# A decoder step on one core: half of the interleaved conditioning weights go to an unsplit stream behind the recurrent gates

## The chip, the cores and the metric

The kernel runs on one core of a Trainium2 chip. The metric is the device time of one execution in microseconds (us). The engines have these names: PE is TensorE's matmul side and PEld its weight loads; DVE is VectorE, ACT is ScalarE, POOL is GpSimd, and SP is the queue that issues most DMAs. An instruction waits on semaphores, and its engine's queue is held until they are reached.

## The reference

One layer of a hybrid decoder on 1024 prompt rows and 64 sample rows (8 sequences of 8), model width 1024. The part that the change touches is the conditioning and the mixer around it:

```python
mod = silu(c) @ w_ada + b_ada            # 9 rows of c, 6*1024 columns
sh_m, sc_m, gt_m, sh_f, sc_f, gt_f = split(mod, 6)
h = rms_norm(x, g_mix) * (1 + sc_m) + sh_m
u_val, u_glu, u_rec, u_y = split(h @ w_in + b_in, 4)
ca = causal_dwconv(u_val * sigmoid(u_glu), width 31)
ya = silu(layer_norm(ca))
cb = causal_dwconv(u_rec, width 4)
hb = rg_lru(cb)                          # two block-diagonal gates, then a scan over time
x = x + gt_m * (concat[ya, hb * gelu(u_y)] @ w_out)
x = x + gt_f * (relu(h2 @ w_up)**2 @ w_down)   # h2 uses sc_f and sh_f
```

The new states of both convolutions and of the recurrence are outputs too.

## The kernel before, in words

Rows of x are tokens in 9 tiles of 128; inside the mixer data is transposed, channels on the partitions and 1088 tokens along the free axis, cut in three chunks of 384, 384 and 320. A float32 product is made from three products of a high and a low part ("split"): ACT copies the raw piece to its high part, POOL subtracts to get the low part, PE multiplies.

The order on every engine is written out by hand; engines meet at semaphores. The program has an opening (norms, the first four of twelve groups of 512 `w_ada` columns, transposes), then **eight steps** of `w_in`, then the **variance stage** of the layer norm, then the **recurrence**, then the output product over 9 tiles, then eight blocks of the MLP.

A step m takes two strips of 128 `w_in` columns (s = 0 and 1), each in three chunks c: 24 products a chunk (PE lines 1472 to 1474 in `strip`). Between the chunks PE does the **conditioning**: one later group of 512 `w_ada` columns a step, in four pieces (`ada_piece`, lines 1364 and 1365, four products of 512 columns each). Each piece is loaded by SP (line 276), copied by ACT (line 590) and subtracted by POOL (line 376). When a group is complete, ACT copies its rows out (`group_rows`, line 576), PE turns them in a product with nine columns (`group_turn`, line 1372), and ACT adds the bias into `mod` (`group_out`, line 581). DVE meanwhile runs the width-31 convolution, one channel tile after another (line 1169), then the width-4 one (line 1146). In the last step PE also forms the mean over channels (`mean`, line 1480).

In the variance stage ACT squares the centred values (`squares`, line 789), PE averages them (line 1480 again, `var_a`) into banks 6 and 7 of PSUM, and ACT takes the root (line 795). In the recurrence PE forms two gates for each of four channel tiles (`recurrent_gates`, line 1567), ACT applies tanh, exp and tanh (`recurrence`, lines 800 to 812), and PE, between them, transposes the convolutions' tails (`turn_state`, line 1557) that ACT copies out (`staged`, line 817). POOL makes low parts of `w_out` and squares of the decay (line 461). PE then turns the mixer's gate rows (`gates`, lines 1589 and 1593) and waits for the first output product (`tile_product`, line 1614), which needs all of the split `ya` and `yb` from ACT and DVE (lines 1243 to 1254). SP loads `w_out` in eight pieces, each after the low part of the piece before it in its slot.

## Time and profile before

| what | value |
|---|---|
| three runs, median (lowest to highest) | 1296.15 us (1293.26 to 1296.56) |
| the profiled execution, its own time | 1296.5 us |
| its span | 1294.7 us |
| PE busy; DVE; ACT; POOL | 92%; 56%; 31%; 29% |
| mean granted clock of PE | 0.957 |

The span is what the trace shows; 1.8 us of the profiled execution lie outside it. PE is busy nearly throughout, but busy time says nothing of the clock: PEclk is the granted clock, 1.00 for 2.4 GHz and 0.50 for 1.2 GHz.

### The profile page before, as it was taken

What the parts mean: (1) busy time and instruction counts of PE and PEld (TensorE: products, weight loads), DVE (VectorE), ACT (ScalarE), POOL (GpSimd) and SP (SyncE); (2) the same over time, 40 slices, a digit from 0 to 9 for tenths busy, and PEclk for the clock granted to TensorE, in tenths of its full rate; (3) what the DMA queues carried; (4) which work ended last, traced back from release to release, by engine and by line L of the source; (5) the groups of instructions that cost most, each with busy time, mean ns of one, the idle gap of its engine ahead of it and who ended that gap; (6) DMA issues with size and microseconds to landing.
All of it is one profiled execution on the core that took longest, in us unless ns stands there. A gap on an engine that the chain in (4) does not pass through costs nothing.

```text
span 1294.7 us, 16511 instructions
## 1 busy us (share of the span) xinstructions
PE 1192.5 (92%) x6175; PEld 1068.0 (82%) x6175; DVE 723.8 (56%) x809; ACT 402.8 (31%) x704; POOL 369.3 (29%) x217
## 2 busy tenths in 40 slices
PE   6798999999723999899999999999999999999996
PEld 2687999997423888888998998998988988988985
DVE  2649699996686455524534534535535435435447
ACT  4752334433791433420320320320310310311322
POOL 0246777652453010410320410410410311311300
PEclk9697999999966999899999999999999999999998
DMA  9533343321204110210210210310300300201102
GB/s 298 163 98 98 98 126 117 109 86 49 68 32 151 37 33 1 82 50 1 78 53 1 81 49 0 90 40 0 97 32 0 97 32 10 87 32 32 49 33 105
DMA packets 74661, 87.26 MB, mean 67 GB/s; under 512 B 3816, under 2 KB 53248, under 8 KB 74627
## 3 DMA queue, kind: packets, MB, share of 16 engines
q1 hardware_dynamic: 72448, 85.21, 21.1%
q10 hardware_dynamic: 2179, 1.61, 0.5%
q8 instruction: 20, 0.33, 0.1%
q14 instruction: 14, 0.11, 0.0%
HBM read 81.72 MB, written 5.08 MB: 67 GB/s over the span
## 4 chain that ended last, share of the span: by engine, by line
PE 85%; DVE 5%; SPq 2%; ACT 2%; POOL 2%; DMA 1%; issue 1%; ACTq 0%; DVEq 0%; POOLq 0%
PE ps L1472 15%; PE ps L1474 14%; PE ps L1473 14%; PE ps L1614 11%; PE ps L1615 11%; PE ps L1617 11%; PE ps L1480 1%; PE ps L1621 1%; PE ps L1620 1%; SPq L265 1%; PE ps L1365 1%; PE ps L1364 1%; DVE tmp_a L1235 1%; DMA x<-in_x_prompt 1%; DVE ga L1232 1%
## 5 line engine op out<-in xcount | busy, mean ns | idle before, releaser
L1472 PE MATMUL ps<-act_hi,w_hi 128*128 128x384 f32 (+1 forms) x1152 | 381.0, 331 | 8.0 <-DVE act_lo L1048 3.9
L1473 PE MATMUL ps<-act_lo,w_hi 128*128 128x384 f32 (+1 forms) x1152 | 378.4, 328 | 0.0
L1474 PE MATMUL ps<-act_hi,w_lo 128*128 128x384 f32 (+1 forms) x1152 | 378.3, 328 | 0.0
L1472 PEld LDWEIGHTS ps<-act_hi,w_hi 128*128 128x128 f32 x1152 | 218.7, 190 | 11.0 <-issue 4.8
L367 POOL TENSOR_TENSOR wb_lo<-raw,wb_hi 128x1024 fp32r<-128x1024 f32 x40 | 99.9, 2506 | 430.0 <-ACT wb_hi L568 403.3
L367 POOL TENSOR_TENSOR w_lo<-raw,w_hi 128x1024 fp32r<-128x1024 f32 x48 | 118.4, 2468 | 363.8 <-ACT w_hi L568 305.7
L1272 DVE TENSOR_TENSOR ps<-ps,gt_p 128x1024 f32<-128x1024 f32 x72 | 88.7, 1233 | 237.6 <-PE ps L1617 237.6
L1473 PEld LDWEIGHTS ps<-act_lo,w_hi 128*128 128x128 f32 x1152 | 218.8, 190 | 1.6
L1474 PEld LDWEIGHTS ps<-act_hi,w_lo 128*128 128x128 f32 x1152 | 218.6, 190 | 0.0
L1614 PE MATMUL ps<-wb_hi 128*128 128x512 f32 x512 | 199.4, 389 | 1.1 <-ACT gt_s L899 1.1
L1615 PE MATMUL ps<-wb_lo,wb_hi 128*128 128x512 f32 x512 | 199.2, 389 | 0.0
L1302 DVE TENSOR_TENSOR relu<-relu 128x384 f32<-128x384 f32 (+1 forms) x96 | 74.7, 778 | 199.3 <-ACT relu L942 199.3
L1617 PE MATMUL ps<-wb_hi,wb_lo 128*128 128x512 f32 x512 | 157.7, 389 | 0.0
L568 ACT ACTIVATE wb_hi<-raw 128x1024 fp32r<-128x1024 f32 x40 | 41.3, 1051 | 364.9 <-PE ps L1621 319.2
L1169 DVE SCALAR_TENSOR_TENSOR ps<-ga,caw,ps 128x1024 f32<-128x1024 f32 x112 | 134.2, 1282 | 0.0
L1614 PEld LDWEIGHTS ps<-wb_hi 128*128 128x128 f32 x512 | 96.1, 188 | 21.1 <-ACT gt_s L899 1.3
L1617 PEld LDWEIGHTS ps<-wb_hi,wb_lo 128*128 128x128 f32 x512 | 96.1, 188 | 20.0
L1615 PEld LDWEIGHTS ps<-wb_lo,wb_hi 128*128 128x128 f32 x512 | 96.1, 188 | 19.7
L942 ACT ACTIVATE relu<-ps 128x384 f32<-128x384 f32 (+1 forms) x96 | 45.2, 471 | 187.6 <-PE ps L1474 178.5
L1274 DVE TENSOR_TENSOR x<-x,ps 128x1024 f32<-128x1024 f32 x72 | 87.9, 1221 | 2.5
L1614 PE MATMUL ps<-wb_hi,act_hi 128*128 128x512 f32 x128 | 51.3, 401 | 39.9 <-DVE stk L1254 39.9
L376 POOL TENSOR_TENSOR aw_lo<-raw_ada,aw_hi 128x1024 fp32r<-128x1024 f32 x32 | 80.2, 2523 | 17.7 <-ACT aw_hi L590 17.7
(224 smaller groups left out, 1298.9 us busy)
## 6 DMA issues: line engine op xcount, KB each, us to landing
raw_ada<-in_w_ada SPq DMA_DIRECT2D x32, 512.0 KB, 3.7
raw<-in_w_up SPq DMA_DIRECT2D x32, 512.0 KB, 4.0
raw<-in_w_down SPq DMA_DIRECT2D x32, 512.0 KB, 3.3
ada<-in_w_ada SPq DMA_DIRECT2D x8, 1024.0 KB, 15.0
x<-in_x_prompt SPq DMA_DIRECT2D x16, 512.0 KB, 8.8
raw<-in_w_in SPq DMA_DIRECT2D x16, 512.0 KB, 4.8
raw<-in_w_out SPq DMA_DIRECT2D x8, 512.0 KB, 3.4
out<-x SPq DMA_DIRECT2D x8, 512.0 KB, 2.6
```

The costliest lines, as they stand in the source:

```text
L367: pool.tensor_tensor(dst, raw[:, slot, :], hi.bitcast(F32), ALU.subtract).then_inc(lo_ready, 1)
L376: pool.tensor_tensor(aw_lo[:, slot, :], raw_ada[:, slot, :], aw_hi[:, slot, :].bitcast(F32), ALU.subtract).then_inc(ada_lo, 1)
L1169: dve.scalar_tensor_tensor(out=out if k == KA - 1 else a, in0=win, scalar=w, in1=a, op0=ALU.mult, op1=ALU.add).then_inc(conva_tap, 1)
L1272: dve.tensor_tensor(src, src, gt_p[:, :], ALU.mult).then_inc(gated, 1)
L1274: dve.tensor_tensor(x2[:, t, :], x2[:, t, :], src, ALU.add).then_inc(rmw_done, 1)
L1302: dve.tensor_tensor(f, r, r, ALU.mult).then_inc(r2_done, 1)
L1472: mm(out, wh, xh, start=(k == 0), stop=False)
L1473: mm(out, wh, xl, start=False, stop=False)
L1474: last = mm(out, wl, xh, start=False, stop=(k == KD - 1))
L1614: mm(out, ah, wh, start=(k == 0), stop=False)
L1615: mm(out, ah, wl, start=False, stop=False)
L1617: last = mm(out, al, wh, start=False, stop=end)
```

## The change

Eight `w_ada` groups were split and interleaved with steps 0 to 7. Now four are: their pieces run one step later (group m-1 in step m, steps 1 to 4, and its turn in the step after). The last four groups, which give the MLP's scale and gate rows, are loaded unsplit in sixteen chunks of 128 columns into a buffer that lies where the strips' high and low weights were, and multiplied as float32 with nine columns each, straight into PSUM bank 7 (`late_piece`): two chunks between the recurrent gates, fourteen behind them. One DVE instruction adds their bias. The squares go to other memory and the first stands in the last step; each variance chunk has a bank of its own; the tails all go through bank 6; the loops over the steps are unrolled.

```diff
+ADA_S = 4
+LATE = ADA_G - ADA0 - ADA_S
+ROW_L = 4 * (ADA0 + ADA_S)
...
-        rs = shared([("h_st", [9, WA], F32)], [("w_hi", [P, 2, D], F32R)])
-        h_st, w_hi = rs["h_st"], rs["w_hi"]
-        w_lo = sb("w_lo", [P, 2, D], F32R)
+        rs = shared([("h_st", [9, WA], F32)], [("ada_late", [P, 4, KD, P], F32)],
+                    [("w_hi", [P, 2, D], F32R), ("w_lo", [P, 2, D], F32R)])
+        h_st, ada_late, w_hi, w_lo = (rs[n] for n in ("h_st", "ada_late", "w_hi", "w_lo"))
...
-        xsq = tmp_b[:, 0:J, :]
+        xsq = lru
...
+            for m in range(2 * J):
+                if m < 2 * J - 1:
+                    nxt, apart = ((m + 1) * P, WA) if m < J - 1 else (2 * WA + (m + 1 - J) * 2 * P, P)
                     for s in range(2):
-                        load_piece(2 * m + s + 1, s, win_v[:, :, bass.ds(nxt + s * apart, P)], True)
-                load_ada(m, 2)
-                load_ada(m, 3)
-                if nxt is not None:
-                    load_ada(m + 1, 0)
-                    load_ada(m + 1, 1)
-
-            with sp.Fori(0, J - 1) as j:
-                step(j, (j + 1) * P)
-            step(J - 1, 2 * WA, P)
-            with sp.Fori(0, J - 1) as j:
-                step(j + J, (j + 1) * (2 * P) + 2 * WA, P)
-            step(2 * J - 1, None)
-            for k in range(KD):
+                        load_piece(2 * m + s + 1, s, win_v[:, :, nxt + s * apart:nxt + s * apart + P], True)
+                if 0 < m <= ADA_S:
+                    load_ada(m - 1, 2)
+                    load_ada(m - 1, 3)
+                if m < ADA_S:
+                    load_ada(m, 0)
+                    load_ada(m, 1)
+
+            def load_late(a):
+
+                for i in range(4):
+                    wait(sp, late_used, 4 * (a - 1) + i + 1)
+                    at = (ADA0 + ADA_S + a) * GW + i * P
+                    sp.dma_start(ada_late[:, i, :, :], wada_v[:, :, at:at + P]).then_inc(late_in[i], 16)
+
+            def load_out(k):
                 load_piece(W_OUT0 + k - 1, k % 2, w_out[0, k * P:(k + 1) * P, :], False)
+
+            load_out(0)
+            load_out(1)
+            sp.wait_ge(strip_a, 2 * J * NC)
+            sp.wait_ge(strip_b, 2 * J * NC)
+            load_late(0)
+            for k in range(2, 6):
+                load_out(k)
+            for a in range(1, LATE):
+                load_late(a)
+            load_out(KD - 2)
+            load_out(KD - 1)
...
+            def step(m):
+                if m < 2 * J - 1:
...
+                if 0 < m <= ADA_S:
+                    split_ada(4 * m - 2, 0)
+                    split_ada(4 * m - 1, 1)
...
-                    pool.wait_ge(ada_evac, ADA_G)
-                    for g, row0 in ((0, M_GTM), (1, M_GTF)):
-                        for k in range(KD):
-                            last = pool.tensor_copy(gt_tok[:, g, k, :].rearrange("p (b t) -> p b t", t=TB),
-                                                    mod[:, row0 + k, 1:9].unsqueeze(2).broadcast_to([P, NB, TB]))
-                    last.then_inc(tails, 1)
-                    pool.wait_ge(ada_tr, ADA_G)
-                    pool.wait_ge(st_tr, 1)
+                    pool.wait_ge(ada_tr, ADA0 + ADA_S)
+                    pool.wait_ge(ada_evac, ADA0 + ADA_S)
+                    sample_gate(0, M_GTM)
...
+            pool.wait_ge(late_mod, 1)
+            sample_gate(1, M_GTF)
...
+                def out_b(c, bank):
+                    if last and c == 2:
+                        squares(0)
+                    gelu_out(c, bank, 2 * q + 1, evac_b)
+                step(q + J + J // 2, out_a, out_b)
...
-                act.activation(rstd[:, t0:t0 + w], ps[:, 6 + c % 2, 0:w], ACT.Sqrt, bias=eps[:, :]).then_inc(sd_done, 1)
+                act.activation(rstd[:, t0:t0 + w], ps[:, 5 + c, 0:w], ACT.Sqrt, bias=eps[:, :]).then_inc(sd_done, 1)
...
-            squares(0)
             squares(1)
             squares(2)
-            act.wait_ge(ada_lo, 4 * 2 * J)
-            w_out_hi(0)
             for c in range(NC):
                 deviation(c)
+            w_out_hi(0)
             w_out_hi(1)
+            recurrence(0)
             staged(0, stage[0:KA - 1, 2, :], 6, KA - 1)
             act.dma_start(ca_prompt[0, 0], stage[0:KA - 1, 2, :]).then_inc(staged_out, 16)
             staged_a(0)
-            recurrence(0)
+            recurrence(1)
             staged_a(1)
-            staged(3, stage[64:64 + KB - 1, 2, :], 7, KB - 1)
+            w_out_hi(2)
+            recurrence(2)
+            staged(3, stage[64:64 + KB - 1, 2, :], 6, KB - 1)
             act.dma_start(cb_prompt[0, 0], stage[64:64 + KB - 1, 2, :]).then_inc(staged_out, 16)
-            recurrence(1)
-            w_out_hi(2)
+            w_out_hi(3)
+            recurrence(3)
             staged(4, stage[32:32 + NB * (KB - 1), 2, :], 6, NB * (KB - 1))
             act.dma_start(cb_sample[0].rearrange("b s c -> (b s) c"),
                           stage[32:32 + NB * (KB - 1), 2, :]).then_inc(staged_out, 16)
...
+            dve.wait_ge(late_used, 4 * LATE)
+            b_late = par[:, C_BADA + ROW_L:C_BADA + 48].unsqueeze(2).broadcast_to([P, 48 - ROW_L, 9])
+            dve.tensor_tensor(mod[:, ROW_L:48, :], ps[:, 7, 0:9 * (48 - ROW_L)].rearrange("p (r c) -> p r c", c=9),
+                              b_late, ALU.add).then_inc(late_mod, 1)
+            dve.wait_ge(ada_evac, ADA0 + ADA_S)
+            dve.wait_ge(late_mod, 1)
             scales(sc_f, M_SCF, C_GFFN)
...
             def var_a(c):
                 pe.wait_ge(sq_done, c + 1)
                 if c == 1:
-                    pe.wait_ge(ada_evac, ADA_G)
-                if c == 2:
-                    pe.wait_ge(sd_done, 1)
-                mean(c, 6 + c % 2, lambda j: xsq[:, j, c * CH:c * CH + CW[c]], var_done)
-
-            def step(m, last=False, late=()):
+                    pe.wait_ge(ada_evac, ADA0 + ADA_S)
+                mean(c, 5 + c, lambda j: xsq[:, j, c * CH:c * CH + CW[c]], var_done)
...
-                        if c == 0 and s == 0:
-                            for i in late:
-                                ada_piece(m - 1, i)
-                            group_turn(m + ADA0 - 1, 7, 0)
-                        for i in ((), (2 * s,), (2 * s + 1,))[c]:
-                            ada_piece(m, i)
+                        if isinstance(m, int) and s == 0 and c == 0 and 2 <= m <= ADA_S + 1:
+                            group_turn(ADA0 + m - 2, 7, 0)
+                        if isinstance(m, int) and c > 0 and m <= ADA_S:
+                            ada_piece(m - 1, 2 * s + c - 1)
...
+            for m in range(1, 2 * J - 1):
                 step(m)
             step(2 * J - 1, True)
...
-                wait(pe, st_cp, n - 1)
+                wait(pe, st_cp, n)
...
+            def late_piece(a, i):
+
+                pe.wait_ge(late_in[i], 16 * (a + 1))
+                at = 36 * a + 9 * i
+                for k in range(KD):
+                    last = mm(ps[:, 7, at:at + 9], ada_late[:, i, k, :], c_t[:, k, :],
+                              start=(k == 0), stop=(k == KD - 1))
+                last.then_inc(late_used, 1)
+
             for c in range(NC):
                 var_a(c)
             pe.wait_ge(sd_done, NC)
             pe.wait_ge(tails, 1)
+            recurrent_gates(0)
             turn_state(0, 6, KA - 1, lambda j: tail_p[:, j, :])
-            turn_state(1, 7, 4 * (KA - 1), lambda j: tail_a[:, j, 0:120])
-            recurrent_gates(0)
+            turn_state(1, 6, 4 * (KA - 1), lambda j: tail_a[:, j, 0:120])
+            recurrent_gates(1)
+            late_piece(0, 0)
             turn_state(2, 6, 4 * (KA - 1), lambda j: tail_a[:, j, 120:240])
+            recurrent_gates(2)
+            late_piece(0, 1)
             pe.wait_ge(tails, 2)
-            turn_state(3, 7, KB - 1, lambda j: tail_bp[:, j, :])
-            recurrent_gates(1)
+            turn_state(3, 6, KB - 1, lambda j: tail_bp[:, j, :])
+            recurrent_gates(3)
             turn_state(4, 6, NB * (KB - 1), lambda j: tail_b[:, j, :])
-            recurrent_gates(2)
-            recurrent_gates(3)
+            for q in range(2, 4 * LATE):
+                late_piece(q // 4, q % 4)
...
-            gates(M_GTM, 4, 6)
+            gates(M_GTM, 4, 2)
...
+                    pe.wait_ge(tails, 4)
                     gates(M_GTF, 6, 4)
...
```

On PE, from the last recurrent gate to the first output product, before (L1567 is a recurrent gate, L1557 a tail's transpose, L1589 and L1593 the gate turns, L1614 the output product):

```order
L1567 MATMUL ps<-ga,wg 128x384 [waits evac_a,convb_tap]
L1567 MATMUL ps<-ga,wg 128x384 [waits evac_a]
L1567 MATMUL ps<-ga,wg 128x320 [waits evac_a]
L1567 MATMUL ps<-ga,wg 128x384 [waits evac_b] x2
L1567 MATMUL ps<-ga,wg 128x320 [waits evac_b]
L1589 MATMUL ps<-ident,mod 128x128 [waits st_cp,tails,evac_b,evac_a]
L1589 MATMUL ps<-ident,mod 128x128 x7
L1593 MATMUL ps<-ident,gt_tok 64x128 x8
L1614 MATMUL ps<-wb_hi,act_hi 128x512 [waits yal_done,hi_ready,yah_done,lo_ready,ylo_done,yhi_done]
```
and in the changed program (there L1566, L1556, L1601, L1605 and L1626; L1574 is a late chunk's eight products):

```order
L1566 MATMUL ps<-ga,wg 128x384 [waits evac_b] x2
L1566 MATMUL ps<-ga,wg 128x320 [waits evac_b]
L1556 MATMUL ps<-ident,tail_b 24x128 [waits st_cp]
L1556 MATMUL ps<-ident,tail_b 24x128 x3
L1574 MATMUL ps<-c_t,ada_late 128x9 [waits late_in2]
L1574 MATMUL ps<-c_t,ada_late 128x9 x7
```
The last late chunk and what follows it, in the changed program:

```order
L1574 MATMUL ps<-c_t,ada_late 128x9 [waits late_in3]
L1574 MATMUL ps<-c_t,ada_late 128x9 x7
L1601 MATMUL ps<-ident,mod 128x128 [waits st_cp,tails,evac_b,evac_a]
L1601 MATMUL ps<-ident,mod 128x128 x7
L1605 MATMUL ps<-ident,gt_tok 64x128 x8
L1626 MATMUL ps<-wb_hi,act_hi 128x512 [waits yal_done,hi_ready,yah_done,lo_ready,ylo_done,yhi_done]
```

Fourteen late chunks, of which the first and the last stand here, have come between the last recurrent gates and the gate turns; each chunk waits for its own load.

On ACT, the end of the last step and the variance stage, before (L677 moves the end of a strip's last chunk out, L576 and L581 are the group's rows, L789 squares, L795 is the root, L568 a high part of `w_out`):

```order
L677 ACTIVATE gel<-ps,par 128x64
L576 ACTIVATE ada_rows<-ps 128x512 [waits ada_used]
L581 ACTIVATE mod<-ps,par 128x9 [waits ada_tr]
L581 ACTIVATE mod<-ps,par 128x9 x3
L789 ACTIVATE tmp_b<-conv_a 128x4x384 [waits ada_used,xc_done,strip_b,k_done]
L789 ACTIVATE tmp_b<-conv_a 128x4x384 [waits xc_done]
L789 ACTIVATE tmp_b<-conv_a 128x4x320 [waits xc_done]
L568 ACTIVATE wb_hi<-raw 128x1024 [waits raw_in0,ada_lo]
L795 ACT_TABLE_LOAD
L795 ACTIVATE rstd<-ps,eps 128x384 [waits var_done] x2
L795 ACTIVATE rstd<-ps,eps 128x320 [waits var_done]
L568 ACTIVATE wb_hi<-raw 128x1024 [waits raw_in1]
```
and in the changed program (there L688 and L689, L770, L801 and L580):

```order
L686 ACTIVATE gel<-ps,par 128x384 [waits strip_b] x2
L770 ACTIVATE lru<-conv_a 128x4x384 [waits ada_used,xc_done,strip_b]
L688 ACTIVATE gel<-ps,par 128x256
L689 ACTIVATE gel<-ps,par 128x64
L770 ACTIVATE lru<-conv_a 128x4x384 [waits ada_used,xc_done,k_done]
L770 ACTIVATE lru<-conv_a 128x4x320 [waits ada_used,xc_done]
L801 ACT_TABLE_LOAD
L801 ACTIVATE rstd<-ps,eps 128x384 [waits var_done] x2
L801 ACTIVATE rstd<-ps,eps 128x320 [waits var_done]
L580 ACTIVATE wb_hi<-raw 128x1024 [waits raw_in0]
L580 ACTIVATE wb_hi<-raw 128x1024 [waits raw_in1]
```
The group's rows are gone from the front of the squares. The first square stands ahead of the last move out of a strip, and carries that move's wait for the strip. Both high parts of `w_out` now follow the roots.

On SP, the loads behind the steps, before (L271 is a load of `w_in` or `w_out`, L265 the reload of x):

```order
L276 DMA raw_ada<-in_w_ada 128x2x512 [waits ada_lo] x2
L271 DMA raw<-in_w_out 128x1024 [waits lo_ready] x8
L265 DMA x<-in_x_prompt 128x1024 [waits yah_done,yal_done,ylo_done,yhi_done]
L265 DMA x<-in_x_prompt 128x1024 x7
L265 DMA x<-in_x_sample 64x1024
L271 DMA raw<-in_w_up 128x8x128 [waits lo_ready] x2
```
and in the changed program (there L276 and L270; L313 is a late chunk):

```order
L276 DMA raw<-in_w_out 128x1024 [waits lo_ready] x2
L313 DMA ada_late<-in_w_ada 128x8x128 [waits strip_b,strip_a]
L313 DMA ada_late<-in_w_ada 128x8x128 x3
L276 DMA raw<-in_w_out 128x1024 [waits lo_ready] x4
L313 DMA ada_late<-in_w_ada 128x8x128 [waits late_used] x12
L276 DMA raw<-in_w_out 128x1024 [waits lo_ready] x2
L270 DMA x<-in_x_prompt 128x1024 [waits yah_done,yal_done,ylo_done,yhi_done]
L270 DMA x<-in_x_prompt 128x1024 x7
L270 DMA x<-in_x_sample 64x1024
```
Four late chunks stand behind the first two pieces of `w_out`, and twelve ahead of its last two.

## Rows read from the trace of the kernel before

**Rows 1.** windows by stage: us, busy of each engine (x instructions), PEclk, DMA share, GB/s.
```profile
core 0 of [0], span 1294.7 us
...
139.00:316.50 177.50, 177.50 (x1033) 170.31 (x1031) 161.46 (x134) 64.39 (x118) 116.76 (x75) 1.00 0.33 98
...
368.00:408.00 40.00, 0.38 (x4) 0.14 (x2) 39.06 (x37) 23.34 (x32) 19.00 (x12) 0.54 0.08 26
```

**Rows 2.** timeline of PE at the first step after the opening: start, us, what [idle before].
```profile
98.25 0.66 PE L1472 MATMUL ps<-act_hi,w_hi 128*128 128x384 f32 x1 [3.81 <-ACT w_hi L746]
...
111.33 1.88 PE L1372 MATMUL ps<-pick,ada_rows 128*128 128x9 f32 x8 [4.97 <-ACT ada_rows L576]
...
113.06 0.67 PE L1472 MATMUL ps<-act_hi,w_hi 128*128 128x384 f32 x1
```

**Rows 3.** timeline of PE inside step 1, then the group turns of steps 2 and 3.
```profile
124.26 0.39 PE L1364 MATMUL ps<-aw_hi,stk 128*128 128x512 f32 x1
...
125.19 0.34 PE L1472 MATMUL ps<-act_hi,w_hi 128*128 128x384 f32 x1
...
143.10 0.95 PE L1372 MATMUL ps<-pick,ada_rows 128*128 128x9 f32 x8
...
143.91 0.43 PE L1472 MATMUL ps<-act_hi,w_hi 128*128 128x384 f32 x1
...
171.47 0.95 PE L1372 MATMUL ps<-pick,ada_rows 128*128 128x9 f32 x8
```

**Rows 4.** timeline of DVE, the starts of two tiles of the long convolution.
```profile
147.68 1.35 DVE L1161 TENSOR_SCALAR ps<-ga,caw,par 128x1024 f32 x1 [11.26 <-POOL ga L393]
...
188.94 1.35 DVE L1161 TENSOR_SCALAR ps<-ga,caw,par 128x1024 f32 x1 [0.79 <-DVE conv_a L1172]
```

**Rows 5.** chain that ended last, start, us, what: a mean product of the last step.
```profile
291.15 2.58 PE ps L1480 x8
```

**Rows 6.** timeline of ACT from the last strip to the first gate.
```profile
315.79 0.47 ACT L676 ACTIVATE gel<-ps,par 128x256 f32<-128x256 f32 x1 [3.86 <-PE ps L1474]
...
319.08 4.03 ACT L789 ACTIVATE tmp_b<-conv_a 128x1536 f32<-128x1536 f32 x3
...
331.29 0.53 ACT L795 ACTIVATE rstd<-ps,eps 128x320 f32<-128x320 f32 x1 [1.57 <-PE ps L1480]
...
331.71 1.05 ACT L568 ACTIVATE wb_hi<-raw 128x1024 fp32r<-128x1024 f32 x1
...
334.74 1.28 ACT L800 ACT_TABLE_LOAD   x1 [0.46 <-PE ps L1567]
...
336.04 0.90 ACT L800 ACTIVATE tmp_a<-ps,hb 128x768 f32<-128x768 f32 x1
```

**Rows 7.** windows of PE's clock, columns as in the first group.
```profile
40.00:42.00 2.00, 2.00 (x12) 2.00 (x11) 2.00 (x3) 2.00 (x6) 0.00 (x0) 0.50 1.12 353
...
110.00:112.00 2.00, 0.67 (x4) 0.67 (x4) 2.00 (x3) 1.75 (x3) 2.00 (x3) 0.50 0.98 256
...
408.00:412.00 4.00, 3.77 (x9) 3.03 (x10) 0.28 (x2) 0.00 (x0) 0.00 (x0) 0.50 0.71 255
```

**Rows 8.** timeline of PE, the gate turns and the first output product.
```profile
361.55 3.75 PE L1589 MATMUL ps<-ident,mod 128*128 128x128 f32 x16 [4.38 <-ACT tmp_a L803]
...
365.24 3.14 PE L1593 MATMUL ps<-ident,gt_tok 128*64 128x128 f32 x16
...
408.23 0.77 PE L1614 MATMUL ps<-wb_hi,act_hi 128*128 128x512 f32 x1 [39.85 <-DVE stk L1254]
```

**Rows 9.** page section 6, loads of 512-byte runs: KB each, us to landing.
```profile
raw<-in_w_in SPq DMA_DIRECT2D x16, 512.0 KB, 4.8
```

**Rows 10.** a window in which one such load lands; columns as in the first group.
```profile
642.00:643.00 1.00, 1.00 (x9) 1.00 (x8) 0.83 (x1) 0.97 (x3) 1.00 (x1) 1.00 1.14 343
```

**Rows 11.** timeline of DVE, start and end of the recurrence's last part.
```profile
367.71 1.29 DVE L1232 SCALAR_TENSOR_TENSOR ga<-tmp_a,ga 128x1088 f32<-128x1088 f32 x1
...
407.92 0.21 DVE L1254 TENSOR_TENSOR stk<-gel,stk 128x64 fp32r<-128x64 f32 x1
```

135 lines of the change are left out of this document (54 added, 81 removed).

## The prediction

> **What bounds the kernel now.** I read the page's slices first, then the chain of work that ended last, then windows by stage, and last the timelines of PE, ACT and DVE around each join. The span is 1294.7 us; the profiled execution took 1296.5 us, so 1.8 us lie outside the span, and it is 0.35 us above the median of the runs. The sum below is made against 1296.5.
>
> From 139 to 316.5 us PE is busy for all of the 177.5 us, at a granted clock of 1.00: the steps are bound by PE, and an instruction taken out of PE's row there comes off the end [rows 1]. From 368 to 408 us it is the other way round: PE does nothing, DVE is busy for 39.06 of 40 us, and PE's first output product then follows an idle time of 39.85 us that a DVE write of `stk` ended [rows 1, 8]. So there are two bounds, PE in the steps and the chain through ACT, POOL and DVE in the recurrence. Behind 408 us the edit touches only small waits (the MLP's gate rows), and I take that part as unchanged.
>
> **The steps.** One piece of conditioning is four products, which hold PE from 124.26 to 125.19, so a piece costs 0.93 us. A group's turn, eight records for four products, takes from 143.10 to 143.91, which is 0.81 us. The turns of steps 2 and 3 lie 28.37 us apart, so a step without pieces and turn is 28.37 - 4 x 0.93 - 0.81 = 23.84 us, and its first chunk (384 of 2 x 1088 columns) about 4.2 us [rows 3].
>
> Step 1 now begins at 98.25 us behind an idle time of 3.81 us [rows 2]. Two pieces that stood ahead of that idle time move away, but the wait is for the low part of the weights, which POOL makes behind the first gate product; so I leave the start at 98.25. Before, PE ran out of conditioning pieces in this step, sat idle for 4.97 us for ACT's group rows, and turned them at half rate (the next product is 1.73 us later) [rows 2]. Its step 2 began about 4.2 us ahead of 143.10, at 138.9. After the change step 1 holds four pieces, whose splits have been ordered long before, and no turn: 23.84 + 3.72 = 27.6 us, and I allow 3.5 us for a slow beginning, since PE's clock stood at 0.50 after the similar idle time at 110 us [rows 7]. That gives 129.3 instead of 138.9: **9.6 us**. Bounds: 0 to 6 us for the slow beginning.
>
> Steps 2 to 4 keep four pieces and a turn. Step 5 keeps its turn. Steps 5, 6 and 7 lose four pieces each, 11.2 us, and steps 6 and 7 a turn each, 1.6 us; one piece of these stood behind the last chunk, so the last chunk ends 11.9 us earlier by that. Before, ACT moved it out at 315.79 [rows 6]; now at 315.8 - 9.6 - 11.9 = **294.3**. Can DVE follow? A tile of the long convolution takes 41.26 us, and before the first two were parted by 11.26 us of waiting [rows 4]. With the product of step 1 some 9 us earlier the four tiles close up, and the last ends near 138 + 3 x 41.26 = 262 instead of 147.68 + 3 x 41.26 = 271.5. The mean in step 7 then asks for it at 294.3 less five chunks and the means, near 271. So DVE isn't late, with some 9 us to spare. Unrolling can gain nothing, since PE had no gaps at the loops' ends; I price it at 0, and at most 2 us of loss.
>
> **The variance stage.** Before, from the last move-out to the first tanh it was 336.04 - 315.79 = 20.25 us [rows 6]. The change puts the first square ahead of that move, but the order rows show that it carries the wait for the last chunk, so the square begins in the last step in name only; its 4.03 / 3 = 1.34 us stand behind the chunk [rows 6]. Then three averages at the rate of the mean in step 7, 2.58 us each at most [rows 5], run without waiting for one another's bank, one root 0.53, two high parts of `w_out` at 1.05, and a table load of 1.28 [rows 6]: 1.34 + 7.74 + 0.53 + 2.1 + 1.28 = 13.0 us. The first tanh comes at 307.3, which is 28.7 us earlier. If the averages run at half rate as they did before, 3 to 7 us of that are lost.
>
> **The recurrence, by the y chain.** Before, the last part on DVE began at 367.71, 31.7 us behind the first tanh, and ended at 408.1 [rows 6, 11]. Each tail now goes through bank 6 and waits for the copy of the one before: a round trip on ACT and PE, some 0.5 us each, five times. POOL, on the other side, copies eight gate rows there and not sixteen. I take the two as equal, with -2 to +2.4 us around it. By this chain the first output product would come at 408.2 - 28.7 = 379.5.
>
> **The recurrence, by the late chunks.** The same PE row now holds sixteen chunks, 14 of them between the last gates and the gate turns. A chunk is eight products of nine columns. At full rate it costs 2 x 0.81 = 1.62 us [rows 3]. At half rate, from the group's turn at 111.33 to the next product at 113.06, it costs 2 x 1.73 = 3.46 us [rows 2]. Which rate will be granted is the largest unknown of this sum. At 40 to 42 us PE was busy for all of 2 us, with transposes, at 0.50, and at 110 to 112 us, when a turn began behind idle time, it was at 0.50 too [rows 7]. The turns at full rate stand inside dense strips [rows 3]. The chunks come behind gates with gaps between them, so I take **half rate**, 3.46 us, and keep 1.62 as the other end.
>
> The Trainium skill (TensorE: Matmul & The Clock Gate, section Why this matters for your kernels) asks to keep TensorE busy without gaps to have the full rate, and by that a run of fourteen chunks should be at 2.4 GHz; the window from 40 to 42 us, busy throughout at 0.50, does not agree, and no run here shows a long row of nine-column products. By that rule the result would be the first rival below.
>
> PE ended its last gate at 361.55 - 4.38 = 357.2, which is 21.1 us behind the first tanh [rows 6, 8]. Two chunks now stand between the gates and partly fill its gaps; I take 26 us, so the run starts at 333.3. Fourteen chunks of 3.46 are 48.4 us: 381.7. The loads keep up: one of 512 KB in 512-byte runs takes 4.8 us to land in the median, but its bytes pass at up to 343 GB/s, 1.5 us each with several under way, and four are under way [rows 9, 10]. SP issues the second four behind the sixth piece of `w_out`, which waits for POOL's fourth low part, near the start of the run. The gate turns take 365.24 + 3.14 - 361.55 = 6.8 us [rows 8]: **388.5**. The last two pieces of `w_out` stand behind the late loads in SP's queue, which wait until the twelfth chunk is used, at 333.3 + 10 x 3.46 = 368; they land near 374, and behind them ACT's last `yb` parts and DVE's end near 381, ahead of the turns' end.
>
> **The sum.** The first output product moves from 408.2 to 388.5: 19.7 us. Before, it started cold, at 0.50 from 408 to 412 us [rows 7]; behind the turns it should start warm, which saves about 1.7 us. 1296.5 - 19.7 - 1.7 = 1275.1, and against the median of the runs 1275.
>
> **Rivals.**
> 1. *The late chunks hide.* They run at full rate; 14 x 1.62 = 22.7 us end near 356, and the y chain sets the start at 379.5, cold. Time: 1296.5 - 28.7 = 1268; with the recurrence shorter by 2, 1266. For it: a turn inside a step takes 0.81 us [rows 3]. Against it: the windows at 0.50 [rows 7].
> 2. *The loads pace the run.* They land 4.8 us apart [rows 9]. The twelve behind SP's late issue, at about 334, land until 392; with one chunk and the turns 402.4, so 1296.5 - 5.8 - 1.7 = 1289. Against it: 343 GB/s in the window [rows 10].
> 3. *Slower.* The loads come strictly one at a time, each behind the use of the chunk before: 4.8 + 3.46 = 8.3 us by twelve, 99 us from 334, and the turns: 440. The product starts 32 us late: 1327. It decides from 5.6 us a chunk on ((408.2 - 6.8 - 334) / 12). Against it: four buffers, four semaphores, and SP waits only for the use of the chunk four places back.
> 4. *It does not do what it says.* The steps stay as long as they were because something else than PE sets them (DVE's convolution, the weights' low parts). Then only the variance stage's 7 us are won: the run starts at 336 - 7 + 26 = 355, and with 48.4 and 6.8 us the first product comes at 410, so about no change, 1296. Against it: PE's 177.5 of 177.5 us [rows 1].
>
> **How the numbers follow.** A time within 0.3% of before (4 us) can't be told from no change here. Forecast 0.60, rival 1 0.24, rival 2 0.08, rival 3 0.03, rival 4 0.03, and 0.02 for faster still. The forecast's own range, from the slow beginning, the averages' rate and the start of the run, is 1269 to 1282. The range that holds 8 in 10 takes rival 1 in and stops at rival 2: 1264 to 1288. Faster 0.94, within 0.3% 0.03, slower 0.03.
>
> **What would show it.** In the changed profile: no wait for group rows in step 1, and steps 5 to 7 near 24 us each; the last strip's end near 294; the first square behind it; the first tanh near 307; the fourteen chunks in one run at a granted clock of 0.50 and 3.5 us each; the gate turns directly behind them and the first output product directly behind the turns, with no DVE wait ahead of it. Wrong if the first output product still waits for `stk` (then rival 1), if PE waits for late loads between chunks (2 or 3), or if the last strip ends later than 300.

## The result and the profile after

The changed kernel takes 1271.9 us (median of four runs, 1271.63 to 1273.25) against 1296.4 us (1293.26 to 1296.93): a ratio of 0.9818, with a 95% interval of 0.9801 to 0.9835. The forecast was 1275. The profiled execution has a span of 1270.0 us, 24.7 less than before; the difference is made ahead of the first output product, as a table by step shows (us from the span's start).

| step | before | forecast | measured |
|---|---|---|---|
| step 2 of `w_in` begins | 138.9 | 129.3 | 128.5 |
| last chunk of the steps is out of PE | 315.8 | 294.3 | 293.3 |
| first tanh of the recurrence | 336.0 | 307.3 | 306.2 |
| the row of late chunks begins | | 333.3 | 329.8 |
| it ends | | 381.7 | 380.3 |
| last `stk` of the y chain written | 408.1 | 379.5 | 380.6 |
| first output product | 408.2 | 388.5 | 385.6 |
| from there to the end of the span | 886.5 | 884.8 | 884.4 |

The first tanh comes 29.8 us earlier. The first output product comes only 22.6 us earlier: 7.2 us are given back in the recurrence, where PE's row is now the longest. 2.1 us more lie behind the first output product, which now starts at full clock (its first record takes 0.50 us, against 0.77 before [rows 8]). Together 24.7.

Timeline of PE in the changed kernel (start, us, engine, line, what, number of records, [idle before <- what ended it]); it answers to [rows 2, 3, 8]:

```profile
98.80 0.66 PE L1481 MATMUL ps<-act_hi,w_hi 128*128 128x384 f32 x1 [5.70 <-POOL w_lo L383]
...
128.53 0.34 PE L1481 MATMUL ps<-act_hi,w_hi 128*128 128x384 f32 x1
...
311.89 1.11 PE L1556 MATMUL ps<-ident,tail_a 128*120 128x128 f32 x4 [4.48 <-ACT stage L823]
...
317.69 1.85 PE L1574 MATMUL ps<-c_t,ada_late 128*128 128x9 f32 x16
...
329.78 4.52 PE L1574 MATMUL ps<-c_t,ada_late 128*128 128x9 f32 x32
339.20 41.13 PE L1574 MATMUL ps<-c_t,ada_late 128*128 128x9 f32 x192 [4.90 <-DMA ada_late<-in_w_ada]
380.18 3.62 PE L1601 MATMUL ps<-ident,mod 128*128 128x128 f32 x16
383.73 1.96 PE L1605 MATMUL ps<-ident,gt_tok 128*64 128x128 f32 x16
385.62 0.50 PE L1626 MATMUL ps<-wb_hi,act_hi 128*128 128x512 f32 x1
```

Read it from below. The first output product has no idle time before it: it follows the gate turns, and these follow the late chunks, where before it had waited 39.85 us for DVE [rows 8]. A chunk is 16 records. Two chunks took 4.52 us; then PE stood still for 4.90 us for a load, and twelve more took 41.13 us, 3.43 each.

Timeline of ACT, same columns, which answers to [rows 6]:

```profile
293.25 1.48 ACT L770 ACTIVATE lru<-conv_a 128x1536 f32<-128x1536 f32 x1 [2.93 <-PE ps L1483]
294.64 0.46 ACT L688 ACTIVATE gel<-ps,par 128x256 f32<-128x256 f32 x1
...
306.20 0.90 ACT L806 ACTIVATE tmp_a<-ps,hb 128x768 f32<-128x768 f32 x1
...
372.29 1.06 ACT L580 ACTIVATE wb_hi<-raw 128x1024 fp32r<-128x1024 f32 x1 [14.18 <-DMA raw<-in_w_out]
```

The first square does stand ahead of the last move-out, and PE's last chunk released it. At 372.29 ACT gets the seventh piece of `w_out` behind 14.18 us of waiting. Timeline of DVE, which answers to [rows 11]: one product of the recurrence for the first and for the third channel tile, 1.29 and 3.28 us, and the end of the chain.

```profile
338.44 1.29 DVE L1236 SCALAR_TENSOR_TENSOR ga<-tmp_a,ga 128x1088 f32<-128x1088 f32 x1
...
349.78 3.28 DVE L1236 SCALAR_TENSOR_TENSOR ga<-tmp_a,ga 128x1088 f32<-128x1088 f32 x1
...
380.36 0.21 DVE L1258 TENSOR_TENSOR stk<-gel,stk 128x64 fp32r<-128x64 f32 x1
```

The change did not make the third one long. In the kernel before it was the same:

```profile
379.04 3.27 DVE L1232 SCALAR_TENSOR_TENSOR ga<-tmp_a,ga 128x1088 f32<-128x1088 f32 x1
```

Windows of the changed kernel (stretch; length; busy time of PE, PEld, DVE, ACT, POOL; granted clock; DMA share; GB/s), which answer to [rows 1, 7]:

```profile
139.00:290.00 151.00, 151.00 (x888) 146.32 (x887) 145.45 (x131) 44.83 (x86) 76.98 (x59) 1.00 0.23 67
...
330.00:332.00 2.00, 2.00 (x20) 2.00 (x19) 0.34 (x1) 1.97 (x3) 2.00 (x6) 1.00 0.00 0
332.00:334.00 2.00, 2.00 (x13) 2.00 (x12) 0.00 (x0) 1.97 (x3) 2.00 (x2) 0.58 0.01 4
...
350.00:360.00 10.00, 10.00 (x49) 10.00 (x48) 9.72 (x8) 8.05 (x12) 5.71 (x4) 0.50 0.55 159
...
384.00:386.00 2.00, 2.00 (x18) 1.78 (x17) 0.00 (x0) 1.13 (x2) 0.00 (x0) 1.00 0.89 328
```

PE is still busy in all of the steps. In the row of late chunks it is busy too, for 10.00 of 10.00 us, and yet the clock is at 0.50 (1.2 GHz). It was still at 1.00 from 330 to 332 us, with the first chunk of the row, fell while the second one ran and PE was busy, and came back only in the gate turns.

### The profile page after: what moved, and what is told of

It reads as the page before. It is cut to its first block, busy times and chain, and to the rows that moved or that the text cites. A ratio compares the mean times of both kernels' runs of the same rounds, so it can differ in the third digit from the quotient of the medians.

```text
span 1270.0 us, 16342 instructions
## 1 busy us (share of the span) xinstructions
PE 1212.0 (95%) x6335; PEld 1094.6 (86%) x6335; DVE 708.1 (56%) x810; ACT 382.5 (30%) x668; POOL 326.9 (26%) x201
## 4 chain that ended last, share of the span: by engine, by line
PE 90%; DVE 2%; SPq 2%; ACT 2%; DMA 1%; issue 1%; POOL 0%; ACTq 0%; DVEq 0%; POOLq 0%
PE ps L1481 15%; PE ps L1483 15%; PE ps L1482 15%; PE ps L1626 11%; PE ps L1629 11%; PE ps L1627 11%; PE ps L1574 4%; PE ps L1633 1%; PE ps L1632 1%; PE ps L1489 1%; SPq L270 1%; PE ps L1566 1%; DMA x<-in_x_prompt 1%; SPq L276 1%; PE ps L1374 1%
## 5 line engine op out<-in xcount | busy, mean ns | idle before, releaser
L1626 PE MATMUL ps<-wb_hi 128*128 128x512 f32 x512 | 199.4, 389 | 1.1 <-ACT gt_s L903 1.1
L580 ACT ACTIVATE wb_hi<-raw 128x1024 fp32r<-128x1024 f32 x40 | 41.2, 1051 | 375.0 <-PE ps L1633 319.3
L1626 PEld LDWEIGHTS ps<-wb_hi 128*128 128x128 f32 x512 | 96.1, 188 | 21.1 <-ACT gt_s L903 1.3
L1316 DVE TENSOR_TENSOR wb_lo<-relu,wb_hi 128x384 fp32r<-128x384 f32 (+1 forms) x96 | 51.5, 536 | 7.6 <-ACT stk L952 4.0
L1574 PEld LDWEIGHTS ps<-c_t,ada_late 128*128 128x128 f32 x256 | 49.4, 302 | 5.3 <-DMA ada_late<-in_w_ada 5.0
```

The source lines that it names most:

```text
L1574: last = mm(ps[:, 7, at:at + 9], ada_late[:, i, k, :], c_t[:, k, :], start=(k == 0), stop=(k == KD - 1))
L1626: mm(out, ah, wh, start=(k == 0), stop=False)
```

## The experiments

Each kernel is the changed one with the edit shown. Ratios are to the kernel before, as above (the changed kernel: 0.9818).

**The gate turns behind the fourth chunk.** The theory under test is that PE's row sets the first output product.

```diff
-            for q in range(2, 4 * LATE):
-                late_piece(q // 4, q % 4)
...
-            gates(M_GTM, 4, 2)
+            for q in range(2, 4 * LATE):
+                if q == 4:
...
+                    gates(M_GTM, 4, 2)
+                late_piece(q // 4, q % 4)
```

> The gate turns stand in PE's row behind the fourth late chunk, where PE now waits 4.90 us for loads, and no longer behind the sixteenth. My theory: PE's row of late chunks and turns sets the first output product. The turns can begin once ACT has copied the last tails, near 335.4, and take 5.4 to 6.8 us, so they fill that wait; the twelve chunks (41.1 us) then end near 382 and the first output product follows there, not at 385.6: the time is 1272 - 3.6 = 1268, and the product stands directly behind a chunk. Rival: the y chain sets it (the last stk at 380.4 in the changed kernel was only waiting for nothing better); then the product stays near 385 and the time at 1272. Second rival: the turns, whose products have 128 columns, bring the clock back to 1.00 for the chunks behind them; then the twelve chunks take 20 us and the product waits for stk, at about 380: 1266 or less.

Measured: 1268.4 us, ratio 0.9789 (0.9773 to 0.9806). Timeline of PE:

```profile
335.22 3.75 PE L1598 MATMUL ps<-ident,mod 128*128 128x128 f32 x16 [1.73 <-ACT stage L823]
338.90 2.76 PE L1602 MATMUL ps<-ident,gt_tok 128*64 128x128 f32 x16
341.59 38.98 PE L1574 MATMUL ps<-c_t,ada_late 128*128 128x9 f32 x192
381.19 0.77 PE L1628 MATMUL ps<-wb_hi,act_hi 128*128 128x512 f32 x1 [0.63 <-issue]
```

The turns fill the wait for loads, and the product comes at 381.2 instead of 385.6. The first theory holds, as far as the y chain lets it: the last chunk ended at 380.6 and the last `stk` was written at 381.1, so the two are now level. The second rival had a small part: behind the turns the clock was at 1.00 from 341 to 343 us, but at 0.50 again from 345 on, and the twelve chunks took 38.98 us instead of 41.13, not 20. Now that thin chunks stand directly ahead of it, the product starts cold (0.77 us).

**SP's order.** The late loads go between the `w_out` pieces, each as its buffer comes free.

```diff
...
-            load_late(0)
-            for k in range(2, 6):
-                load_out(k)
-            for a in range(1, LATE):
-                load_late(a)
-            load_out(KD - 2)
-            load_out(KD - 1)
+            for q, k in ((0, None), (1, None), (2, None), (3, None), (0, 2), (0, 3), (4, None), (5, None), (0, 4), (6, None), (0, 5), (7, None), (8, None), (9, None), (10, None), (11, None), (12, None), (0, 6), (13, None), (14, None), (0, 7), (15, None)):
+                if k is None:
+                    load_late(q // 4, q % 4)
+                else:
+                    load_out(k)
```

> Only SP's order is changed: the late loads go between the w_out pieces as their buffers come free, and the last two w_out pieces go between the last late loads. My theory: PE's wait of 4.90 us for late loads goes (the fifth chunk's load is issued near 320 and not at 334), the run ends near 375.4, the turns near 380.8, and the first output product follows there; the last stk comes near 375 instead of 380.4, because ACT no longer waits 14 us for w_out. Time 1272 - 4.8 = 1267. Rival: the loads were not what held PE (the clock or the buffers were), and the product stays near 385: 1272. Rival: SP's waits for POOL's low parts hold late loads back in the new order, PE waits between chunks, and it is slower than 1272.

In a pair, q is the late chunk that is loaded, or k the piece of `w_out`.

Measured: 1267.4 us, 0.9787 (0.9770 to 0.9803). Timeline of PE, then a window, then DVE's timeline:

```profile
330.01 44.91 PE L1571 MATMUL ps<-c_t,ada_late 128*128 128x9 f32 x224
374.76 3.35 PE L1598 MATMUL ps<-ident,mod 128*128 128x128 f32 x16
...
379.94 0.50 PE L1623 MATMUL ps<-wb_hi,act_hi 128*128 128x512 f32 x1
```

```profile
334.00:336.00 2.00, 2.00 (x11) 2.00 (x11) 1.19 (x1) 1.61 (x4) 1.66 (x1) 0.50 0.90 232
```

```profile
371.56 3.41 DVE L1253 TENSOR_TENSOR act_lo<-gel,act_hi 128x1024 fp32r<-128x1024 f32 x1
...
378.91 0.21 DVE L1255 TENSOR_TENSOR stk<-gel,stk 128x64 fp32r<-128x64 f32 x1
```

The wait is gone and the product comes at 379.9. The clock falls to 0.50 all the same, in a row of fourteen chunks that has no wait in it. One half of the expectation failed: the last `stk` came at 379.1 and not at 375, although ACT's longest wait for `w_out` was 4.08 us there, not 14.18. DVE itself is the bound of that chain, busy for 33.1 of the 34 us from 340 to 374, and some of its short instructions are long (3.41 us where others of the shape take 1.21).

**One product of eight.** Is the y chain really that close behind?

```diff
-                for k in range(KD):
+                for k in range(1 if 4 * a + i > 3 else KD):
...
-                              start=(k == 0), stop=(k == KD - 1))
+                              start=(k == 0), stop=(k == (0 if 4 * a + i > 3 else KD - 1)))
```

> The last twelve late chunks keep their loads, waits and signals but do one product of eight (seven eighths of these products are left out, so the MLP's gate and scale rows are not what they should be). My theory: PE's 41 us of chunks set the first output product by only a few us over the y chain. Without them SP's late loads go out close together, the last two w_out pieces are issued near 353 and not at 367, the last stk comes near 375 and the first output product waits for it there, cold: 385.6 - 10 and 2 us lost to the clock, so 1272 - 8 = 1264. Rival: the run of chunks is the whole of it and the y chain is ready far earlier: the product comes near 350 and the time is 1272 - 36 = 1236.

Measured: 1267.5 us, 0.9785 (0.9769 to 0.9802). Timeline of PE:

```profile
358.55 0.60 PE L1574 MATMUL ps<-c_t,ada_late 128*128 128x9 f32 x2 [1.18 <-DMA ada_late<-in_w_ada]
...
378.62 0.77 PE L1626 MATMUL ps<-wb_hi,act_hi 128*128 128x512 f32 x1 [14.16 <-DVE stk L1258]
```

With nearly all of the row's work gone the product comes 7.0 us earlier, waits 14.16 us for `stk`, and starts cold. So the y chain ends at 378.5 with PE out of its way (380.6 in the changed kernel), against the 379.5 of the forecast, and the row of late chunks costs what lies above that: 7.0 us at the product, 4.4 us in the time, since the product now starts cold.

**Filler between the chunks.** What holds the clock?

```diff
+            pe.wait_ge(st_cp, 5)
+            pe.wait_ge(hi_ready, W_OUT0 + 1)
             for q in range(2, 4 * LATE):
                 late_piece(q // 4, q % 4)
+                for _ in range(4):
+                    mm(ps[:, 6, :], wb_hi[:, 0, 0:P], wb_hi[:, 0, 0:512], start=True, stop=True)
```

> Behind each of the fourteen late chunks stand four products of 512 columns that nobody reads (at full rate 4 x 0.23 = 0.93 us). Theory: the half rate of the run comes from the chunks' own thin products, and work in between brings the granted clock to 1.00; a chunk then costs 1.65 + 0.93 = 2.6 us, the twelve 31 us, PE's row ends near 376 and the first output product comes there or at the last stk, 376 to 380: time 1263 to 1267. Rival: the run stays at 0.50 whatever stands between; a chunk costs 3.43 + 1.86 = 5.3 us, the twelve end near 403 and the turns near 408: 1272 + 22 = 1294.

Measured: 1298.5 us, 1.0021 (1.0011 to 1.0030). Timeline of PE, then a window:

```profile
350.50 3.42 PE L1574 MATMUL ps<-c_t,ada_late 128*128 128x9 f32 x16
353.77 2.06 PE L1599 MATMUL ps<-wb_hi 128*128 128x512 f32 x4
```

```profile
350.00:360.00 10.00, 10.00 (x41) 9.24 (x40) 9.72 (x8) 7.54 (x11) 5.20 (x4) 0.50 0.35 103
```

The rival is right: the filler ran at half rate as well, and the kernel lost all it had won. The two waits in front of the row held it back until 335.0, after 5.49 us of idle time, so that here the clock stood at 0.50 from the first chunk. The run shows that this filler does not bring the clock back; whether it would have kept a clock that was still at 1.00 is not shown.

**Wide late products.** The nine columns are read fourteen times over.

```diff
-                    last = mm(ps[:, 7, at:at + 9], ada_late[:, i, k, :], c_t[:, k, :],
+                    last = mm(ps[:, 7, at:at + 126].rearrange("p (r c) -> p r c", c=9), ada_late[:, i, k, :],
+                              c_t[:, k, :].unsqueeze(1).broadcast_to([P, 14, 9]),
```

> Each late product moves its nine columns fourteen times over (126 columns, the extra ones overwritten or unread), everything else as in the changed kernel. The gate turns, 16 records of 128 columns, took 3.62 us at 0.50 and 1.96 us at 1.00 in the changed kernel, so a chunk of 16 records would cost 3.6 or 2.0 us. Theory: it is the thin products that hold the clock at 0.50, and wide ones bring it back as the gate turns did; the twelve chunks then take some 24 to 27 us instead of 41, and the first output product waits for stk at about 378.5, as in the run with few products: 1267 to 1268. Rival: the run stays at 0.50 as it did with filler between the chunks; twelve chunks take 43.4 us, the product comes at 388 and the time is 1274.

Measured: 1267.1 us, 0.9779 (0.9763 to 0.9796). Timeline of PE, then windows:

```profile
339.25 18.43 PE L1574 MATMUL ps<-c_t,ada_late 128*128 128x126 f32 x144 [5.32 <-DMA ada_late<-in_w_ada]
358.27 5.62 PE L1574 MATMUL ps<-c_t,ada_late 128*128 128x126 f32 x48 [0.59 <-DMA ada_late<-in_w_ada]
...
379.10 0.77 PE L1627 MATMUL ps<-wb_hi,act_hi 128*128 128x512 f32 x1 [11.52 <-issue]
```

```profile
340.00:342.00 2.00, 2.00 (x12) 2.00 (x11) 1.97 (x2) 1.98 (x3) 0.00 (x0) 0.50 1.16 305
342.00:344.00 2.00, 2.00 (x14) 2.00 (x14) 1.89 (x4) 1.99 (x4) 1.34 (x2) 0.65 0.93 232
344.00:346.00 2.00, 2.00 (x20) 2.00 (x19) 1.83 (x5) 1.97 (x3) 0.00 (x0) 1.00 0.82 242
```

Fourteen times the columns, and the twelve chunks take 24.6 us (with 0.59 of waiting) instead of 41.1. The row starts at 0.50 behind the wait for loads, is at 1.00 from 344 us on and stays there. Nothing but the width of the products differs from the changed kernel, where the same row stayed at 0.50 to its end. The time is bounded by the y chain (last `stk` at 379.0), as it was with one product of eight.

**The pieces one step earlier, as before.** The largest single term of the forecast (9.6 us) is undone; the late groups stay.

```diff
-                            ada_piece(m - 1, 2 * s + c - 1)
+                            ada_piece(m, 2 * s + c - 1)
...
+                ada_piece(0, 0)
+                ada_piece(0, 1)
                 pe.wait_ge(evac_a, NC)
```

> Only the move of the pieces is undone: the four split groups run in steps 0 to 3 as they did before, and the late groups stay unsplit. My theory: step 1 waits again for the group's rows (4.97 us before), turns them at half rate, and its step 2 begins near 139 instead of 128.5, 10.4 us later; step 4 has no pieces now, 3.7 us less. The last strip ends near 301 instead of 294.6 and the time is 1272 + 6.7 = 1278.6. Rival: the steps are shorter only for having fewer pieces in all, and the early place costs nothing, because the two pieces ahead of step 1 fill an idle stretch: 1272 - 1.9 = 1270.

Measured: 1279.7 us, 0.9878 (0.9862 to 0.9895). Timeline of PE, then of ACT (the first tanh):

```profile
98.19 0.66 PE L1495 MATMUL ps<-act_hi,w_hi 128*128 128x384 f32 x1 [3.82 <-POOL w_lo L385]
...
110.73 1.88 PE L1395 MATMUL ps<-pick,ada_rows 128*128 128x9 f32 x8 [4.43 <-ACT ada_rows L597]
```

```profile
312.56 0.90 ACT L820 ACTIVATE tmp_a<-ps,hb 128x768 f32<-128x768 f32 x1
```

The wait for the group's rows is back, and so is its turn at half rate (1.88 us). Step 1 starts only 0.6 us earlier than in the changed kernel, with the two pieces ahead of it. Where the pieces stand is worth 6.4 us at the first tanh and 7.9 in the time; the forecast's 9.6 less the 3.7 of the pieces that step 4 then loses is 5.9.

**The variance stage as before.** Shared banks, and the first square behind the last move-out.

```diff
+                if c == 2:
+                    pe.wait_ge(sd_done, 1)
-                mean(c, 5 + c, lambda j: xsq[:, j, c * CH:c * CH + CW[c]], var_done)
+                mean(c, 6 + c % 2, lambda j: xsq[:, j, c * CH:c * CH + CW[c]], var_done)
...
-                    if last and c == 2:
-                        squares(0)
...
+            squares(0)
             squares(1)
```

> Two edits are undone together: the variance chunks share banks 6 and 7 again (the third waits for the first root), and the first square stands behind the last move-out. My theory: neither is what shortened the stage from 20.25 to 11.56 us; the third average began at about 300.2, and the first root was done at 299.7, so the bank costs under 0.5 us, and the square comes 0.8 us later because two short move-outs stand ahead of it. First tanh about 0.8 us later, 1272.5 to 1273. The 8.7 us came from the last group's rows, turn and move-out that no longer stand between the last strip and the squares, and from PE's clock, which stayed at 1.00. Rival: the banks and the place of the square are the gain: 1272 + 8.7 = 1280.

Measured: 1273.0 us, 0.9827 (0.9811 to 0.9844). Timeline of ACT:

```profile
293.06 0.47 ACT L688 ACTIVATE gel<-ps,par 128x256 f32<-128x256 f32 x1 [2.93 <-PE ps L1482]
...
306.58 0.90 ACT L804 ACTIVATE tmp_a<-ps,hb 128x768 f32<-128x768 f32 x1
```

From PE's last chunk to the first tanh it is 13.5 us, against 12.95 (306.20 - 293.25) in the changed kernel and 20.25 before [rows 6]. These two parts of the change are worth 0.6 us together.

**Three of four conditioning products left out.** How much room has DVE behind the steps?

```diff
-                ada(i, 6, aw_hi[:, i % 2, :], aw_lo[:, i % 2, :], ada_used)
+                mm(ps[:, 6, :], stk[:, 2 * i, :], aw_hi[:, i % 2, 0:GW], start=(i == 0), stop=(i == 3)).then_inc(ada_used, 1)
```

> Three of the four products of each of the sixteen pieces in steps 1 to 4 are left out (so four groups of the conditioning are wrong); the loads, copies, subtractions and signals stay. PE's row is shorter by 16 x 0.70 = 11.2 us. My theory: DVE's long convolution has 9.7 us to spare in the changed kernel (it ended at 260.7, the mean asked for it at 270.4), so the mean waits about 1.5 us for it and the last strip ends near 285: time 1262. Rival: the convolution moves up with the steps, nothing waits, and the last strip ends at 283.4: 1260.7. Rival on the other side: something else sets the steps (POOL's low parts, ACT) and the strips end later than 288: over 1265.

Measured: 1273.5 us in one run. Nothing is won; the rival on the other side is right, by way of ACT. Timeline of ACT, then of PE:

```profile
240.53 1.06 ACT L778 ACTIVATE conv_a<-conv_a,par 128x64 f32<-128x64 f32 x4 [8.18 <-DVE conv_a L1171]
```

```profile
243.54 0.64 PE L1481 MATMUL ps<-act_hi,w_hi 128*128 128x320 f32 x1 [4.50 <-ACT gel L686]
```

In step 6 ACT waits for DVE's sum of the samples of the fourth convolution tile before it moves a chunk out, and PE waits for ACT. In the changed kernel (DVE, then ACT) there was no such wait:

```profile
238.14 2.21 DVE L1171 TENSOR_REDUCE conv_a<-smp_prod  x1
```

```profile
242.69 1.07 ACT L778 ACTIVATE conv_a<-conv_a,par 128x64 f32<-128x64 f32 x4 [2.56 <-PE ps L1483]
```

That sum was written at 240.35 and ACT asked at 242.69: 2.3 us of room, not the 9.7 that the mean has.

**The same, with that sum at the third tap of the tile.**

```diff
-            def conv_a_tile(j):
+            def conv_a_tile(j, at=KA // 2):
...
-                        if k == KA // 2:
+                        if k == at:
...
-            with dve.Fori(0, J) as j:
+            with dve.Fori(0, J - 1) as j:
                 dve.wait_ge(ga_ready, 2 * j + 3)
                 conv_a_tile(j)
+            dve.wait_ge(ga_ready, 2 * J + 1)
+            conv_a_tile(J - 1, 2)
```

> As the run with few conditioning products (three of four left out in steps 1 to 4), and DVE sums the samples of the last convolution tile at its third tap and not at its sixteenth, 14 us earlier (near 224 instead of 238); DVE's work stays the same. In the run before, PE stood still for 4.50 us in step 6 behind ACT, and ACT for 8.18 us behind that sum. Theory: that wait, with the slow clock behind it, is what ate the 11.2 us; with the sum early, PE's row closes up, only the 2.9 us of waits for POOL's low parts and the group's rows remain, the mean asks for the convolution near 262 and finds it done, the last strip ends near 285 and the time is 1272 - 8.3 = 1264. Rival: the last strip is held by something else too (the convolution's end, the next low parts), and nothing is won: over 1270.

Measured: 1263.5 us, 0.9758 (0.9742 to 0.9774): 10 us less than the one run without the earlier sum, and 8.4 less than the changed kernel. In PE's timeline the mean finds the convolution done, with no wait of its own:

```profile
262.29 2.74 PE L1491 MATMUL ps<-conv_a,mean_w 128*128 128x384 f32 x8
```

One dependency had eaten most of the 11.2 us that PE's row is shorter by.

**Three edits together.** Wide late products, the late loads among the `w_out` pieces, and the low parts of pieces 4 to 7 on DVE instead of POOL; then the same with the gate turns held back.

```diff
...
+            def w_out_lo(k):
+                dve.wait_ge(lo_ready, W_OUT0 + k)
+                dve.wait_ge(hi_ready, W_OUT0 + k + 1)
+                dve.tensor_tensor(wb_lo[:, LO_SLOT[k], :], raw[:, k % 2, :], wb_hi[:, k, :].bitcast(F32),
+                                  ALU.subtract).then_inc(lo_ready, 1)
...
+            pe.wait_ge(ylo_done, 2)
             gates(M_GTM, 4, 2)
```

> Three edits on the changed kernel: late products of 126 columns, late loads between the w_out pieces, and the low parts of w_out pieces 4 to 7 made by DVE and not by POOL. With PE out of the way (late run and turns done near 363) the y chain alone sets the first output product. My theory: DVE stands still for 2.0 to 2.2 us beside each of POOL's four low parts there (a DVE instruction of 1.29 us took 3.28 to 3.31, one of 1.21 took 3.41, one of 0.21 took 2.42), 8.2 us in all, while the same subtraction on DVE costs 1.21 each, 4.9 in all: the last stk comes 3.3 us earlier than 379.1, at 375.8, the first product with it, cold (2.1 us lost to the clock): 1272 - 9.8 + 2.1 = 1264. Rival: DVE's long instructions have another cause than POOL's work, the four subtractions are simply added, and stk comes near 384: 1272 or slower.

Measured: 1263.9 us, 0.9754 (0.9741 to 0.9767). Timeline of DVE, then of PE:

```profile
349.48 1.29 DVE L1237 SCALAR_TENSOR_TENSOR ga<-tmp_a,ga 128x1088 f32<-128x1088 f32 x1
...
354.68 1.22 DVE L1227 TENSOR_TENSOR wb_lo<-raw,wb_hi 128x1024 fp32r<-128x1024 f32 x1
```

```profile
374.96 0.77 PE L1634 MATMUL ps<-wb_hi,act_hi 128*128 128x512 f32 x1 [12.31 <-DVE stk L1263]
```

The instruction that took 3.28 us takes 1.29, DVE does the four subtractions at 1.22 each, and `stk` is done at 374.9, 4 us earlier than in the runs with one of the other two edits alone (379.1 and 379.0).

> As the kernel before in this call, and the gate turns wait until DVE has written the second yb low part, about 7 us before the last stk. Theory: the turns (5.4 us from a cold start) end shortly before the last stk, and the first output product starts at a granted clock of 1.00 instead of 0.50, which saves the 2.1 us of a cold start: 1262 to 1262.5. Rival: the short idle time between the turns and the product is enough to lose the clock again, or the turns run past the last stk: 1264 or more, no better than without the wait.

Measured: 1261.2 us (1260.85 to 1261.8), 0.9734 (0.9721 to 0.9748): the fastest of all. Timeline of PE:

```profile
368.99 3.75 PE L1609 MATMUL ps<-ident,mod 128*128 128x128 f32 x16 [10.14 <-DVE stk L1263]
372.67 2.43 PE L1613 MATMUL ps<-ident,gt_tok 128*64 128x128 f32 x16
375.23 0.47 PE L1635 MATMUL ps<-wb_hi,act_hi 128*128 128x512 f32 x1
```

The product starts no earlier, but warm (its first record takes 0.47 us, against 0.77 in the run before): 2.7 us won by work that only changed its time. The other runs bear this out: from the start of the first output product to the end of the span it is 886.4 to 887.5 us in the four whose product starts cold (the gate turns behind the fourth chunk, one product of eight, wide products, three edits together), and 884.3 to 885.0 us in the changed kernel and the seven runs in which it starts at full clock.

## Why the prediction was right, point by point

*The steps.* Step 1 came out as forecast: its start was 98.80 for 98.25, behind a wait for a low part as said, its slow beginning cost less than the 3.5 us allowed (15 products at 0.32 us against 0.17, 2.2 us), and step 2 began at 128.5. The undone move shows that this term is the place of the pieces, and not their number. The last chunk left PE 1.0 us ahead of the forecast. That unrolling the loops is worth nothing, as priced, is not shown by a run of its own.

*DVE's room.* Here a step failed, though nothing hung on it this time. The forecast looked at the mean only and named 9 us. That holds for the mean (asked at 270.4, ready at 260.7), but ACT in step 6 asks DVE for a sum 28 us earlier, and there the room was 2.3 us. A few more microseconds off PE's row would have come back as that wait.

*The variance stage.* 12.95 us for 13.0. The square began "in the last step in name only", as said, and banks and square are worth 0.6 us. The stage is 7.3 us shorter, and the timelines say where. 3.3 us stood ahead of the squares before (319.08 - 315.79 [rows 6]): 0.6 of them are the move-outs that the first square now precedes, the rest the last group's rows and turn. 3.0 us lie in the averages, whose 24 records took 7.55 us at full clock instead of 10.53. 1.0 us lies between the last root and the first tanh, where ACT copied two tails out. Beyond the 0.6 us, this split is read from the timelines and not shown by a run. Before, a window of the averages shows a clock of 0.66:

```profile
320.00:330.00 10.00, 9.28 (x20) 5.35 (x21) 3.13 (x2) 6.50 (x7) 0.00 (x0) 0.66 0.00 0
```

*The late chunks.* The place, the half rate (3.43 us a chunk for 3.46) and the order behind them were right: the row and the turns bound the first product, and the y chain, forecast at 379.5, or near 381 by way of the last `w_out` pieces, was ready at 380.6, 5 us ahead of it. But several terms were mis-sized, in both directions, and that the sum came so close is partly luck. "The loads keep up" failed: SP issued the next twelve at 333.9, as forecast, but the first of them landed 5.3 us later, with both chunks at hand used up, and PE stood still for 4.90 us. Against that the row began 3.5 us early (the last gates came 23.6 us behind the first tanh, not 26), its first two chunks took 4.5 us and not 6.9, the other twelve 0.4 us less, and the turns 5.4 and not 6.8. Sum: 4.9 - 3.5 - 2.4 - 0.4 - 1.4 = -2.8, and the product came 2.9 us early. In the y chain "some 0.5 us" for each tail that goes through the one bank was too little: PE once waited 4.48 us there for ACT's copy. It did little harm, for DVE's last part began 32.2 us behind the first tanh (338.44 - 306.20), against 31.7 before.

*The clock.* The rate was right, but the reason given for it was not, and that is luck too. The forecast took half rate because the chunks come "behind gates with gaps between them". From 320 to 332 us PE was busy without a gap and the clock was at 1.00, the row's first chunk included; it fell while PE was busy with the second. It fell in the same way in the run with SP's order changed, where no wait stands in the row at all. With 126 columns in each product the row came from 0.50 to 1.00 although it began behind 5.32 us of idle time. The Trainium skill (TensorE: Matmul & The Clock Gate, section Why this matters for your kernels) advises keeping TensorE busy without gaps, to get to the full rate and stay there. The rows go against it as a sufficient rule: PE was busy for all of 350 to 360 us at 0.50, with the thin chunks and with filler among them. Rival 1, the late chunks at full rate, came about only in the run with wide products, and there the time was 1267.1, inside that rival's 1266 to 1268.

## What to carry to other kernels

When work moves from a stage that PE bounds to one that it does not, add up PE's new row there at the clock that this kind of work gets, and compare it with the chain beside it: here 36 us of PE work cost 4.4 us, because the other chain ended that close. Room on an engine is to be read at each thing that others ask of it, and not only at the last: here 2.3 us at a sum in step 6, 9.7 us at the mean. And where the last wait ahead of a dense stage is fixed, put work that has to be done anyway right before its end, so that the stage starts warm.
